# One hybrid block on one core: the order of the attention heads, the chunk states and the recurrence steps

## What is computed

```python
proj = rms_norm(h, norm1_g) @ w_in
y_rwkv = rwkv7_group(...)       # 8 heads of 64; S = S*decay + sa x (kk*a) + v x k, y = S r, token by token
y_diff = diff_attn_group(...)   # 4 heads, two softmaxes each: (softmax(s1) - lam * softmax(s2)) @ v, block of 128 rows
h = h + concat([y_rwkv, y_diff]) @ w_out
h = h + cross_attn(rms_norm(h), rms_norm(mem), wq, wkv, wo)
h = h + moe(rms_norm(h))        # top 4 of 32 experts, 12 MB of float32 weights each
out = rms_norm(h, final_g)
```

## Time and profile before

| | us |
|---|---|
| runs (3) | median 1312.25 (1312.08 to 1313.76) |
| profiled execution, its own time | 1312.39 |
| span of its records | 1310.6 |
| TensorE busy in the span | 1228.3 (94%) |
| VectorE, ScalarE, GpSimd busy | 320.4 (24%), 198.5 (15%), 14.5 (1%) |
| DMA | 445.28 MB, mean 340 GB/s |
| a 1 MB weight load, issue to landing (median, wkv_x) | 4.9 |
| chain that ended last | PE 64%, DMA 28%, DVE 4%, ACT 2% |

### The profile page before, as it was taken

The page is one execution under the profiler, slowest core; times in us unless marked ns, Lnnn a source line. Parts: engine busy times, 40 slices in busy tenths (PEclk is TensorE's granted clock), DMA queues, the critical chain, the costliest instruction groups (busy, mean ns, idle before and its releaser), DMA issues.

```text
span 1310.6 us, 15377 instructions
## 1 busy us (share of the span) xinstructions
PE 1228.3 (94%) x6440; PEld 590.3 (45%) x6440; DVE 320.4 (24%) x775; ACT 198.5 (15%) x371; POOL 14.5 (1%) x52
## 2 busy tenths in 40 slices
PE   6999979999979999999999999999999999999996
PEld 5788857788843333333333333333333333333322
DVE  4544446112141121211212111111211112112113
ACT  2311342012021111111111111111111111111111
POOL 4000000000000000000000000000000000000000
PEclk9999969999979999999999999999999999999998
DMA  8333101582469999999999999999999999999992
GB/s 314 121 137 109 37 2 70 204 338 99 195 281 389 409 432 432 432 432 431 432 432 432 432 432 431 432 432 432 432 432 432 432 432 432 432 432 432 432 426 96
DMA packets 27315, 445.28 MB, mean 340 GB/s; under 512 B 8144, under 2 KB 8528, under 8 KB 10128
## 3 DMA queue, kind: packets, MB, share of 16 engines
q1 hardware_dynamic: 22640, 444.27, 80.4%
q10 hardware_dynamic: 4640, 0.53, 0.3%
HBM read 443.47 MB, written 1.31 MB: 339 GB/s over the span
## 4 chain that ended last, share of the span: by engine, by line
PE 64%; DMA 28%; DVE 4%; ACT 2%; issue 1%; DVEq 0%; SPq 0%; ACTq 0%
PE ps L1227 20%; DMA ring<-in_moe_w 15%; PE ps L1254 12%; DMA arena<-in_moe_w 12%; PE ps L822 9%; PE ps L842 6%; PE ps L1161 4%; PE ps L1179 3%; DMA ring<-in_wq_x 1%; PE ps L1167 1%; PE ps L1217 1%; ACT arena L796 1%; PE ps L989 1%; PE ps L849 1%; PE ps L1172 1%
## 5 line engine op out<-in xcount | busy, mean ns | idle before, releaser
L1227 PE MATMUL ps<-ring,arena 128*64 128x512 f32 x1216 | 268.7, 596 | 14.1 <-DMA ring<-in_moe_w 14.1
L1227 PE MATMUL ps<-arena 128*64 128x512 f32 x832 | 183.4, 595 | 10.3 <-DMA arena<-in_moe_w 10.3
L1227 PEld LDWEIGHTS ps<-ring,arena 128*64 128x64 f32 x1216 | 84.8, 137 | 196.9 <-issue 174.0
L1254 PE MATMUL ps<-ring,arena 128*64 128x512 f32 x640 | 141.7, 595 | 0.7
L1739 DVE TENSOR_SCALAR arena<-ps 128x512 f32<-128x512 f32 x32 | 22.1, 692 | 452.8 <-PE ps L1227 452.8
L792 ACT ACTIVATE arena<-arena 128x512 f32<-128x512 f32 x32 | 20.1, 629 | 714.4 <-DVE arena L1739 714.4
L1227 PEld LDWEIGHTS ps<-arena 128*64 128x64 f32 x832 | 58.0, 137 | 134.3 <-issue 117.6
L822 PE MATMUL ps<-arena,ring 128*128 128x256 f32 x480 | 107.0, 385 | 2.4 <-DMA ring<-in_wq_x 1.3
L822 PEld LDWEIGHTS ps<-arena,ring 128*128 128x128 f32 x480 | 92.1, 193 | 16.6 <-issue 4.0
L1254 PE MATMUL ps<-arena 128*64 128x512 f32 x384 | 85.0, 595 | 0.0
L1254 PEld LDWEIGHTS ps<-ring,arena 128*64 128x64 f32 x640 | 47.7, 137 | 81.4 <-issue 80.2
(11 more groups left out here) (267 smaller groups left out, 849.1 us busy)
## 6 DMA issues: line engine op xcount, KB each, us to landing
ring<-in_moe_w SPq DMA_DIRECT2D x55, 4096.0 KB, 38.4
arena<-in_moe_w SPq DMA_DIRECT2D x38, 4096.0 KB, 38.4
ring<-in_w_in SPq DMA_DIRECT2D x13, 1024.0 KB, 4.8
ring<-in_moe_w SPq DMA_DIRECT2D x6, 2048.0 KB, 10.8
ring<-in_wkv_x SPq DMA_DIRECT2D x8, 1024.0 KB, 4.9
ring<-in_w_out SPq DMA_DIRECT2D x4, 1024.0 KB, 4.7
ring<-in_wq_x SPq DMA_DIRECT2D x4, 1024.0 KB, 9.2
ring<-in_wo_x SPq DMA_DIRECT2D x4, 1024.0 KB, 4.7
```

What stands on the lines that cost most here:

```text
L1227: ins = t.matmul(ps[c * BLK:(c + 1) * BLK, 4 + b, :], xeT[:, col:col + BLK], w[:, f0:f0 + 512], start=False, stop=(k == KC - 1), skip_grou ...
L1254: ins = t.matmul(ps[c * BLK:(c + 1) * BLK, 7, :], acT[:, col:col + BLK], w[:, f0:f0 + 512], start=(k == 0), stop=(k == KC - 1), skip_group ...
```

## The change

Unit 1's scores stand between yz0 and Rh1, and the first four chunk states ahead of unit 0's values; unit 2's scores come before the turn of unit 1; unit 2's turn and values lie in recurrence steps 3 and 4 in the place of filler parts, and so four filler parts and not two are left behind the loop. The ynT turns stand ahead of kv4 and kv5. VectorE drains yz1 (a copy of its own) and takes the first half of Rh before the first combine; its combine(2) stands behind step 1. ScalarE's exps(1) comes before the copy of at0, unit 0's outputs behind the first four chunk states. Each unit has its own exponentials' buffer, and scratch buffers move.

```diff
-        soft = [cut(XT0 + 1024, 2, 512)] * 2 + [side(11, 2, 2, 512)[:, 1]]
+        soft = [cut(XT0 + 1024, 2, 512)] + [side(11, 2, 2, 512)[:, n] for n in range(2)]
...
-        osq = side(11, P)
+        osq, ysq = cut(XT0 + 1024, P), side(11, HD)
...
-        place("at0", 2)
-        place("od0", 3)
-        place("sc10", 0)
-        place("sc11", 1)
+        for u in (1, 2):
+            place(f"sc{u}0", 0)
+            place(f"sc{u}1", 1)
+        for u in range(3):
+            place(f"at{u}", 2)
+            place(f"od{u}", 3)
         for c in range(NCH - 1):
             place(f"PP{c}", (4, 5, 6, 7)[c % 4])
-        place("sc20", 0)
-        place("sc21", 1)
-        place("at1", 2)
-        place("od1", 3)
-        place("at2", 3)
-        place("od2", 2)
...
-                if u == 1:
-                    product(act, "at0")
...
             exps(0)
-            for i in range(NT):
-                copy(Y0[:, i, :], f"yz{i}")
+            copy(Y0[:, 0, :], "yz0")
+            exps(1)
             taken(act, "bo1")
             copy(atT[0][:, :], "at0")
-            exps(1)
-            head_outputs(0)
             for c in range(4):
                 copy(PhiPsi[:, c, :, :], f"PP{c}", four)
+            copy(atT[1][:, :], "at1")
+            head_outputs(0)
             exps(2)
             for c in range(4, NCH - 1):
                 copy(PhiPsi[:, c, :, :], f"PP{c}", four)
-            copy(atT[1][:, :], "at1")
             head_outputs(1)
...
-                link(s.activation(osq[:, 0:HD], Yn[:, 0, hh * HD:(hh + 1) * HD], ACT.Square, accum_out=st[:, 16 + hh:17 + hh]))
+                link(s.activation(ysq[:, :], Yn[:, 0, hh * HD:(hh + 1) * HD], ACT.Square, accum_out=st[:, 16 + hh:17 + hh]))
...
                 done(ins, f"yz{i}")
-            turn_weights(0)
-            values(0)
-            scores(1)
-
-            for i in range(NT):
+                if i == 0:
+                    scores(1)
+
+            def states(i):
...
-                if i == 0:
-                    scores(2)
+
+            turn_weights(0)
+            states(0)
+            values(0)
+            scores(2)
             turn_weights(1)
+            states(1)
             values(1)
-            turn_weights(2)
-            values(2)
...
-                        next(filler)
+                        if c == 3:
+                            turn_weights(2)
+                        elif c == 4:
+                            values(2)
+                        else:
+                            next(filler)
...
             turned("kv3", memT)
+            for i in range(NT):
+                pe.wait_ge(sem("yn_ready"), i + 1)
+                turn4(f"ynT{i}", [Yn[:, i, m * P:(m + 1) * P] for m in range(4)])
             natural("kv4", memT)
             natural("kv5", memT)
-            for i in range(NT):
-                pe.wait_ge(sem("yn_ready"), i + 1)
-                turn4(f"ynT{i}", [Yn[:, i, m * P:(m + 1) * P] for m in range(4)])
...
-            for i in range(NT):
+            def take_rh(i):
                 o = four(product(dve, f"Rh{i}"))
                 drain(v.tensor_tensor(RhT[:, :, i * P:(i + 1) * P], o, AR[:, :, i, 1, :], ALU.add), f"Rh{i}")
 
+            take_rh(0)
...
             combine(0)
+            take_rh(1)
             score_max(1)
+            drain(v.tensor_copy(Y0[:, 1, :], product(dve, "yz1")), "yz1")
             combine(1)
             score_max(2)
-            combine(2)
...
                 dve.sem_inc(sem("S_ready"), 1)
+                if c == 1:
+                    combine(2)
                 if c == 3:
                     outputs(0)
```

More of the change, by code:

```diff
@@ L1072, in _ @@
             turned("kv3", memT)
-            natural("kv4", memT)
-            natural("kv5", memT)
             for i in range(NT):
@@ L1077, in _ @@
                 turn4(f"ynT{i}", [Yn[:, i, m * P:(m + 1) * P] for m in range(4)])
+            natural("kv4", memT)
+            natural("kv5", memT)
             t.sem_inc(sem("mixers_through"), 1)
```

## The result

Changed kernel: median 1297.42 us (1295.69 to 1299.71, 4 runs) against 1312.28 (1312.08 to 1313.76): ratio 0.988, 95% interval 0.9861 to 0.990, so 15.7 us less (13 to 18); the two medians lie 14.9 apart. A second set with nothing edited gave 1298.36 (6 runs) against 1311.62 (18 runs): 0.9896 (0.9877 to 0.9916), 13.6 us less. The profiled execution is the slowest of the first four, at 1299.71.

A forecast was written before the change was run, and what follows sets the result against it. Bound by a dependency chain at the heads, then TensorE. The loop starting 15.1 us earlier, less new waits and one low stretch, plus shorter waits at out0, summed to 12.8 us off 1312.39: 1299.7 written, range 1297.0 to 1305.5.

The forecast's parts named there:

- a dependency chain at the heads, then TensorE itself: Stretch up to out0: small head pieces wait on ScalarE or VectorE, partly at half clock, then TensorE's own work binds.
- The last 144 records ... hence 1.6: 174.0. values(1): 175.0: Second chunk states ahead of the loop: 1.6 us at full clock, ending at 174.0, then values(1) ending at 175.0.
- The forecast wait of about 3 us, ended by exps: Ahead of the recurrence loop: TensorE idles 3.1 us until ScalarE's exps(2) drain banks 0 and 1 at 178.0.
- One low stretch: Around S1 and its filler: one stretch of 3.4 us at half clock after the new wait, costing 1.7 us.
- The rival of more low clock: One to three more half-clock stretches of 1.7 us each around the new waits: 1301.3 to 1304.8 us, chance 0.25.
- The waits at S4, S6, yn and in out0: TensorE waits in the loop and behind it: 1.0, 2.2, 0.3 and 0.3, and 0.7 us.
- two head pieces and 3.9 us of waits and slow clock stand in their place: Recurrence loop: 23.8 us against 23.0 before, though two fillers lighter, because of these pieces and waits.
- I take everything behind out0 as rigid: From out0 to the kernel's end: what out0 ends earlier, the kernel ends earlier; 12.8 us passes through.
- The rival that the saving doesn't arrive: Transfers behind out0 keep their time and the 16.6 us wait shrinks or grows to match: 1312 us, chance 0.03.
- (c) with a rounding of the hand-overs: Case of no low stretch, 1298.0 us, chance 0.12; with rounding it sets the range's low end, 1297.0.
- The slower case: Clock falls in the 3.1 us wait and stays low through the loop: up to 1331 us, chance 0.03.
- The sentence of the Trainium skill: ynT turns ahead of kv4: transposes don't count as busy, so one more low stretch, 1.7 us: 1301.3, chance 0.05.

The follow-up runs named there:

- b2: Kernel before, with two unused 128x512 products ahead of scores(2) and two ahead of the second group of chunk states: 1312.14 us, ratio 1.0003 to before.
- a0: Changed kernel again, nothing edited: 1298.36 us, ratio 0.9896 to the kernel before.
- c6: Changed kernel plus two unused products behind the logits and two ahead of the first gather in the router stage: 1299.09 us, ratio 0.9903 to before.
- a2: Changed kernel with unit 2's turn, values and combine put back ahead of the recurrence, filler parts back in steps 3 and 4: 1300.75 us, ratio 0.9917 to before.
- c5: Changed kernel with the reciprocal root moved behind state 6 and three moves in ScalarE's list: 1294.20 us, ratio 0.9862 to before.
- c2a: Changed kernel plus two unused 128x512 products inside the second group of chunk states, ahead of its last quarter: one run, 1297.45 us.
- c2b: Changed kernel plus two unused 128x512 products ahead of the whole second group of chunk states: one run, 1295.40 us.
- a1: Changed kernel with the ynT turns put back behind kv5: 1303.29 us, ratio 0.9944 to before.
- c7: Changed kernel with late root, ScalarE's three moves, and unused products ahead of the second chunk states and in the router stage: 1290.39 us, ratio 0.9843 to before.

## Why the prediction was right in its mechanism, and where it failed

- **"a dependency chain at the heads, then TensorE itself"**, and the slow clock with it: right for the chain. For the clock it was too much to price the slow pieces at half: in b2 the clock is up at scores(2) and the states, the order old, and the time is the same.
- **The working, step by step.** Forecast and changed kernel: states begin 167.75, 167.92; values(0) end 171.0, 171.2; second states 172.4, 172.86; loop 178.1, 179.12; S1 179.75, 180.28; S4 190.2, 190.65; S6 197.8, 198.26; end of the loop 201.95, 202.5; kv4 218.15, 219.16; first expert unit 240.3, 241.36. All of these are within 1.1 us.
- **"The last 144 records ... hence 1.6: 174.0. values(1): 175.0"**: wrong, 177.1 and 179.1. The stop of 2.0 us was not in the sum (the row of before shows it only as 133 records and the rest later), and values(1) ran at half clock. The forecast wait of about 3 us, ended by exps, is therefore not there. It cost little, since exps(2) would have held the loop until 178.2 anyway: the sum's wait and the real stop lie over each other. That the loop's start came out within 1.0 us is in this part luck.
- **One low stretch**: there were two of 3.4 us in both traces (176 to 182.8 in the first, 176.5 and 197 in a0), one in c6. The rival of more low clock came true with one stretch more, 1.7 us, in two of three traces.
- **The waits at S4, S6, yn and in out0**: 1.01, 2.17, 0.38 and 0.18, 0.56, against 1.0, 2.2, 0.3 and 0.3, 0.7.
- **Unit 2 between the steps** "two head pieces and 3.9 us of waits and slow clock stand in their place": right, and a2 shows that the move as a whole is worth what its low clock is.
- **"I take everything behind out0 as rigid"**: right for the mechanism: the issue itself moves by 21 us over the fourteen traces, and issue to end by no more than 1053.5 to 1057.5 in thirteen of them (1059.2 in c5). The rival that the saving doesn't arrive is out.
- **The step that failed is the size of that same term.** The sum put the part behind out0 at no difference, and the range gave it no room: its low end is "(c) with a rounding of the hand-overs", 1.0 us below the case without low clock ahead of out0. The runs show that this part came out 0.1 to 3.7 us shorter with the changed list: 1057.5 and 1056.6 us in the two traces of before, 1056.5 and 1056.5 in the two of the changed kernel, 1054.4 and 1053.8 in c2a and c2b, whose list is the same behind the issue. 1.5 us of it goes with the fall at the logits and some with the rest of the low clock in the router stage, and a0 lost 3 us again at the last transfer. A changed kernel with 13.7 us of low clock there and a short last wait comes by these rows to 156.4 + 84.4 + 1054.1 + 1.8 = 1296.7, an estimate just below the range. The faster runs of the first set (1295.69 and 1296.98) have no trace, so that they are of this kind is not shown.
- **The base of the sum.** It set an expected list against one execution of before and took that one as the kernel. The stretch from Rh was 96.8 us in it and 98.1 in the second trace, so by the means the gain ahead of out0 is 13.1 and not the 11.9 of the first pair, against 12.8 in the sum. Both kernels move by several us from run to run, and the unknown was laid only into the new kernel's clock.
- **The slower case**, a clock that does not come back: it came back at 183, during the first full filler, as the row of before had it.
- **The ynT turns and the clock.** The clock is 1.00 from 182.8 to 241 in the changed kernel, through the turns and their waits. The sentence of the Trainium skill (TensorE: Matmul & The Clock Gate, Part 4: PE-mode transpose), by which kv4 would have started slow, is not borne out by this trace; a1, where the turns stand ahead of a 3.09 us wait, did fall behind them, and there turns and wait can't be told apart.

## What to carry to other kernels

When lists written by hand are reordered, lay the new lists against the old durations engine by engine: here that gave all events within 1.1 us but the end of the second states and values(1) (3.1 and 4.1 off), and it showed beforehand which wait takes the place of the one removed (ScalarE's exps, then the root behind the squares). Those waits are the next edits: c7, with them moved off the state chain and with the extra products, is another 7 us faster by the ratios. Take the range from two or more executions of the kernel, not from one, and give the part that the change doesn't touch its own scatter in it. Count low clock only where TensorE is not waiting for somebody else anyway.

## What was not expected of the hardware

- Two groups of small matmuls (32x64, 192 and 144 records) close together seem to outrun the loading of TensorE's instructions: a stop of 1.2 to 2.0 us after record 128 of the second group in all seven traces with these two groups as in the changed list, always in the same place and 2.2 to 3.0 us behind an instruction packet, gone when 1.9 us of wide work stood inside the group (c2a).
- Idle TensorE time ahead of out0 of 3.09 us left the clock at 1.00 in both traces of before, and was followed by 3.4 us at 0.50 in a1 (at 234) and in b2 (at 245.5). The same wait has both outcomes.
- A kernel on one core whose four runs lay within 1.7 us in the first set spread over 7.8 us in 52.
- The wait for the last transfer of an expert, 1.5 us in most traces, was 2.0 to 3.0 in three of fourteen, with half clock behind it: 2 to 3 us more at the end of 1300.
